# Attention of a two-layer streaming encoder: packed queries, two jobs on their own rows of the array, values stationary in column halves, a negated minimum as the exponent's bias

## The reference, cut to what matters

```python
# A: 6 query heads of 64, 2 key heads, window of 128 tokens, a learned sink per head
m = jnp.maximum(s.max(-1, keepdims=True), sink)
e = jnp.exp(s - m)
p = e / (e.sum(-1, keepdims=True) + jnp.exp(sink - m))
# B: 4 heads, two softmax maps per head of 32 columns each, values of 64
p = jax.nn.softmax(jnp.where(mask, s, NEG_INF), axis=-1)
w = p[:, :, 0] - lam * p[:, :, 1]
o = rms_norm(jnp.einsum('bhqk,bkhe->bqhe', w, v), subln) * (1.0 - lam_init)
# C: 6 heads of 64, causal, logits plus a difference of cumulated forget gates
s = s + (cum_q[..., :, None] - cum_k[..., None, :])
p = jax.nn.softmax(jnp.where(mask, s, NEG_INF), axis=-1)
```

## Time and profile before

| | us |
|---|---|
| three timed executions | 3512.90, 3514.46, 3520.23 (median 3514.46) |
| span of the profiled execution | 3514.1 |
| PE busy in it | 3223.0 (92%) |
| PE weight loads busy | 2884.4 (82%) |
| DVE busy | 1718.7 (49%) |
| ACT busy | 1076.7 (31%) |
| POOL busy | 54.3 (2%) |

### The profile page before, as it was taken

How to read it: one execution, slowest core, us unless ns; L and a number is a source line. 1 busy time by engine, 2 the same in 40 slices (tenths; PEclk the granted TensorE clock), 3 DMA queues, 4 the chain that set the end, 5 groups by cost and what they waited for, 6 DMA issues and landing times. The chain is left out here.

```text
span 3514.1 us, 50348 instructions
## 1 busy us (share of the span) xinstructions
PE 3223.0 (92%) x18146; PEld 2884.4 (82%) x18146; DVE 1718.7 (49%) x4094; ACT 1076.7 (31%) x2321; POOL 54.3 (2%) x32
## 2 busy tenths in 40 slices
PE   0699899998899999999969997999898999999999
PEld 0589777786789999999958896777777999999998
DVE  0444378643244544545445445785434454454454
ACT  1332276553221111111123225665423111111111
POOL 0000010000000000000000001010000000000000
PEclk9899999998999999999989998999998999999999
DMA  7244544333021111111024445525132111111111
GB/s 170 79 138 133 161 122 106 88 82 116 18 66 36 41 49 36 53 37 36 24 92 124 132 136 138 131 69 137 35 94 59 44 36 54 36 36 54 36 36 60
DMA packets 368396, 274.96 MB, mean 78 GB/s; under 512 B 128546, under 2 KB 336366, under 8 KB 368186
## 3 DMA queue, kind: packets, MB, share of 16 engines
q1 hardware_dynamic: 368218, 272.70, 27.5%
HBM read 195.84 MB, written 78.62 MB: 78 GB/s over the span
## 5 line engine op out<-in xcount | busy, mean ns | idle before, releaser
L1515 DVE TENSOR_TENSOR x<-x,ffn_down 128x512 f32<-128x512 f32 x792 | 509.4, 683 | 0.0
L1537 DVE TENSOR_TENSOR ffn_xn<-ffn_xn,ffn_up 128x384 f32<-128x384 f32 x132 | 73.1, 554 | 758.1 <-ACT ffn_xn L1482 758.1
L418 PE MATMUL ffn_up<-ffn_h_hi,ffn_hi_g 128*128 128x384 f32 x1056 | 360.3, 341 | 15.2 <-DVE ffn_h_lo L243 10.5
L419 PE MATMUL ffn_up<-ffn_h_lo,ffn_hi_g 128*128 128x384 f32 x1056 | 359.7, 341 | 0.0
L420 PE MATMUL ffn_up<-ffn_h_hi,ffn_lo_g 128*128 128x384 f32 x1056 | 359.4, 340 | 0.0
L418 PE MATMUL ffn_up<-ffn_h_hi,ffn_hi_u 128*128 128x384 f32 x1056 | 355.2, 336 | 3.2 <-DVE ffn_lo_u L243 3.2
L420 PE MATMUL ffn_up<-ffn_h_hi,ffn_lo_u 128*128 128x384 f32 x1056 | 354.8, 336 | 0.0
L419 PE MATMUL ffn_up<-ffn_h_lo,ffn_hi_u 128*128 128x384 f32 x1056 | 354.8, 336 | 0.0
L991 PE MATMUL att_S<-att_kT,att_qT 128*128 128x512 f32 (+3 forms) x864 | 322.9, 490 | 33.1 <-DMA att_qT<-scratch_qkT 25.9
L1482 ACT ACTIVATE ffn_xn<-ffn_up 128x384 f32<-128x384 f32 x132 | 64.9, 491 | 861.1 <-PE ffn_up L420 861.1
L418 PE MATMUL prj_acc<-prj_w_hi,prj_h_hi 128*128 128x384 f32 (+2 forms) x864 | 318.8, 369 | 0.0
(11 more groups left out here) (173 smaller groups left out, 5352.5 us busy)
## 6 DMA issues: line engine op xcount, KB each, us to landing
ffn_raw_g<-in_w_gate SPq DMA_DIRECT2D x44, 512.0 KB, 4.0
ffn_raw_u<-in_w_up SPq DMA_DIRECT2D x44, 512.0 KB, 5.1
ffn_raw_d<-in_w_down SPq DMA_DIRECT2D x44, 512.0 KB, 5.1
scratch_qkv<-prj_nat SPq DMA_DIRECT2D x72, 192.0 KB, 1.9
prj_w_raw<-in_w_in SPq DMA_DIRECT2D x64, 192.0 KB, 2.6
scratch_qkv<-prj_nat SPq DMA_DIRECT2D x36, 256.0 KB, 2.1
att_kT<-scratch_qkT SPq DMA_DIRECT2D x16, 576.0 KB
att_vn<-scratch_qkv SPq DMA_DIRECT2D x16, 576.0 KB, 8.4
```

Of the source, the lines that this page charges most:

```text
L418: pe.matmul(out, l_hi, r_hi, start=first, stop=False)
L419: pe.matmul(out, l_hi, r_lo, start=False, stop=False)
L1515: dve.tensor_tensor(x, x, down[:, (q * ND + n) % 4, :], ALU.add).then_inc(added, 1)
L1537: dve.tensor_tensor(a32[:, b, :], sg[:, b, :], up[:, b, 1, 0:384], ALU.mult).then_inc(gated, 1)
```

## The change

`Group` pairs become `Step`s. A step holds two jobs: in A and C the two heads of a query tile, in B the two maps of one head. A group has 9 steps in A and C and 18 in B. Step u does what unit u did, in the same iteration pattern; `values` runs once per query tile (a pair) for both heads.

- Queries are packed: `qT` holds one copy, the two jobs' queries on rows 0 to 63 and 64 to 127 (in B on quarters of 32 rows). Nothing is padded and POOL's clearing of `qT` is gone.
- `score` (L1070) multiplies each job on its own rows alone, alternating between the two jobs by chunk of 512 columns, into different banks of `S`. A step of up to 512 columns uses one half of each buffer, so that two such steps fit; a larger one waits for all earlier reductions.
- The mask in C takes four products on half the rows (L1078) where each pair of jobs had two.
- `values` (L1147): a 128x64 block of `vn` is stationary, the 128 columns of `pT` stream, the two heads alternate and write to partitions 0 to 63 and 64 to 127 of `O`. The output is born transposed.
- The normalization moves: POOL copies the inverse sums to 64 columns per head (`widen`, L1018), PE transposes that (L1112), DVE copies it (L1290) and multiplies `O` by it (L1269 `finish`), in chunks of 4, 4 and 1 tiles. The final transposes, their copies, and the whole detour of the sample tile are gone. B's norm is done in the same layout (L1116, L1121, L1216, L1314).
- The reduction stores minus the biased score and takes a minimum, whose start is minus the sink; the result is the exponent's bias as it stands (scale -1 in the exponent). In A a constant column beside the scores makes the sink's term part of the sum. `s` has four buffers.
- The past keys' copies move from ACT to DVE (L1286).
- SP: four more constant loads at the phase's start; the store of a group's output is issued one group later, behind the loads.

```diff
+        self.heads = (0, 1) if h is None else (h, h)
+        self.turned = 2 if h is None else 1
+        self.blocks = [(r, x) for r in range(self.turned) for x in range(g.n_blocks(i))]
+        self.chunks = -(-len(self.blocks) // 4)
+        self.left = 300 * g.j + 2 * P - self.n if g.kind == "A" else 0
+        self.sinks = 1 if g.kind == "A" else 0
...
+    for st in steps:
+        big = st.n > 512
+        half.append(0 if big or not half or steps[st.index - 1].n > 512 else 1 - half[-1])
+        before_it.append(max((x.index for x in steps[:st.index] if big or x.n > 512 or half[x.index] == half[-1]), default=-1))
+
+    def scores(st, r):
+
+        at = half[st.index] * 512
+        return S[:, r, at:at + st.n]
...
+                    for m in range(2):
+                        sp.dma_start(qT[m * HEAD:(m + 1) * HEAD, b, :], t["qkT"][g.q_row(m):g.q_row(m) + HEAD, :]).then_inc(sem, 16)
+                else:
+                    sp.dma_start(qT[:, b, :], t["qkT"][g.q_row(0):g.q_row(0) + P, :]).then_inc(sem, 16)
...
+            def store(g):
+                if g.kind == "B":
+                    sp.wait_ge(sub_done, 3 * (g.j + 1))
+                else:
+                    sp.wait_ge(finished, 3 * (g.index + 1))
+                sp.dma_start(t["mixT"][g.tile * P:(g.tile + 1) * P, :], mixT[:, g.index % 2, :]).then_inc(mix_stored[g.index % 2], 16)
...
-            for b in range(2):
-                pool.memset(qT[:, b, 0:2, :], 0.0).then_inc(q_zeroed[b], 1)
-            for g in groups:
+            def zero_past(g):
                 if g.index:
-                    pool.wait_ge(scored, jobs_to[g.index * UG])
+                    pool.wait_ge(scored, 2 * first[g.index])
                 pool.memset(qpast[:], 0.0).then_inc(qpast_zeroed, 1)
-                if 1 <= g.index < NG - 1 and fresh(groups[g.index + 1]):
-                    pool.memset(qT[:, (g.index + 1) % 2, :, :], 0.0).then_inc(q_zeroed[(g.index + 1) % 2], 1)
+
+            def widen(g, c):
+                a, e = CHUNKS[c]
+                number = 3 * g.index + c
+                by = 2 if g.kind == "B" else 1
+                at = 2 * pairs[g.index * T + a][2][0].index
+                each_head = inv[:, at:at + 2 * by * (e - a):by].unsqueeze(2).broadcast_to([P, 2 * (e - a), HEAD])
+                pool.wait_ge(inv_ready, chunk_end(g, c) + 1)
+                if number >= 2:
+                    pool.wait_ge(turned, place["spread", (number - 2) // 3, (number - 2) % 3] + 1)
+                pool.tensor_copy(wide[:, number % 2, 0:(e - a) * P].rearrange("p (x d) -> p x d", d=HEAD), each_head).then_inc(widened, 1)
...
+                if before_it[u] >= 0:
+                    pe.wait_ge(biased, 2 * before_it[u] + 2)
...
-                    out, q = S[:, job % 2, :], qT[:, b, m, i * P:(i + 1) * P]
-                    if i < TP:
-                        k0, n = g.keys(i)[0] * P, g.n_cols(i)
-                        for c in range(0, n, 512):
-                            w = min(512, n - c)
-                            last = pe.matmul(out[:, c:c + w], q, kT[:, b, k0 + c:k0 + c + w], start=True,
-                                             stop=not (g.kind == "C" and c + w == n))
-                        if g.kind == "C":
-                            last = pe.matmul(out[:, n - P:n], ident_b[:], mask_b[:], start=False, stop=True)
...
+                k0 = g.keys(i)[0] * P
+                for c in range(0, st.n, 512):
+                    w = min(512, st.n - c)
+                    final = c + w == st.n
+                    for r, m in enumerate(st.maps):
+                        rows_of = slice(m * g.D, (m + 1) * g.D)
+                        made = pe.matmul(scores(st, r)[:, c:c + w], qT[rows_of, b, i * P:(i + 1) * P],
+                                         kT[rows_of, b, k0 + c:k0 + c + w], start=True, stop=not (g.kind == "C" and final))
+                        if final and g.kind != "C":
+                            made.then_inc(scored, 1)
...
+                    for part in range(2):
+                        for r in range(2):
+                            rows_of = slice(r * HEAD, (r + 1) * HEAD)
+                            made = pe.matmul(scores(st, r)[:, st.n - P:st.n], ident_b[rows_of, part, :], mask_b[rows_of, part, :],
+                                             start=False, stop=(part == 1))
+                            if part:
+                                made.then_inc(scored, 1)
 
...
+                def out(h):
+                    return O[h * HEAD:(h + 1) * HEAD, number % 2, at:at + P]
+
+                def weights(h, x):
+                    block = x + h * g.n_blocks(i)
+                    return pT[:, pair % 2, block * P:(block + 1) * P]
...
-                        last = pe.matmul(O[:, u % 2, 0:HEAD], pT[:, u % 2, x * P:(x + 1) * P], vn[:, b, kt, v],
-                                         start=(x == 0), stop=(x == len(ks) - 1))
+                        for h in range(2):
+                            made = pe.matmul(out(h), vn[:, b, kt, h * HEAD:(h + 1) * HEAD], weights(h, x),
+                                             start=(x == 0), stop=(x == len(ks) - 1))
...
-                    act.wait_ge(bias_ready, job + 1)
-                    act.activation(p[:, u % 3, r, 0:n], s[:, job % 2, 0:n], ACT.Exp, bias=bias[:, job:job + 1],
-                                   accum_out=total[:, job:job + 1]).then_inc(exped, 1)
-                    if g.kind == "A":
-                        head = g.j + 3 * h
-                        act.activation(esink[:, job:job + 1], sink[:, head:head + 1], ACT.Exp, bias=bias[:, job:job + 1]).then_inc(sink_ready, 1)
+                    act.wait_ge(turned, place["p", u - 3, steps[u - 3].chunks - 1] + 1)
+                for r in range(2):
+                    job = 2 * u + r
+                    act.wait_ge(biased, job + 1)
...
-                    dve.tensor_tensor_reduce(s[:, job % 2, 0:n], S[:, job % 2, 0:n], extra_row, 1.0, -3e38, ALU.add, ALU.max, mx[:, one]).then_inc(biased, 1)
-                    dve.wait_ge(biased, job + 1)
-                    if g.kind == "A":
-                        head = g.j + 3 * h
-                        dve.tensor_scalar(bias[:, one], mx[:, one], sink[:, head:head + 1], -1.0, ALU.max, ALU.mult).then_inc(bias_ready, 1)
-                    elif g.kind == "B":
-                        dve.tensor_scalar(bias[:, one], mx[:, one], -1.0, None, ALU.mult).then_inc(bias_ready, 1)
-                    else:
-
-                        own = k["cumq"][:, i, 2 * g.j + h:2 * g.j + h + 1]
-                        then(dve.tensor_tensor(mx[:, one], mx[:, one], own, ALU.add))
-                        dve.tensor_tensor(bias[:, one], own, mx[:, one], ALU.subtract).then_inc(bias_ready, 1)
...
+                    if u >= 2:
+                        dve.wait_ge(exped, job - 3)
+                    h = st.heads[r]
+                    extra_row = (add_s[:, b, h, 0:st.n] if i == TP else add_p[:, b, h, 0:st.n] if g.kind == "C"
+                                 else add_p[:, b, h, g.width - st.n:g.width])
+                    floor = neg_sink[:, g.j + 3 * h:g.j + 3 * h + 1] if g.kind == "A" else 3e38
+                    dve.tensor_tensor_reduce(s[:, job % 4, st.left:st.left + st.n], scores(st, r), extra_row, -1.0, floor,
+                                             ALU.add, ALU.min, nmax[:, one]).then_inc(biased, 1)
...
+                if c == 0 and g.index >= 2:
+                    dve.wait_ge(mix_stored[g.index % 2], 16 * (g.index // 2))
+                dve.wait_ge(multiplied, g.index * T + e)
+                dve.wait_ge(dve_took, taken[place["spread", g.index, c]])
+                dve.tensor_tensor(mixT[:, g.index % 2, a * P:e * P], O[:, number % 2, 0:(e - a) * P],
+                                  spread[:, number % 2, 0:(e - a) * P], ALU.mult).then_inc(finished, 1)
```

476 lines of the change are left out of this document (251 added, 225 removed).

## The result

Measured side by side, the changed kernel takes 3418.7 us (median of 4 runs, 3416.8 to 3429.1), the kernel before 3514.9 (3512.9 to 3520.2): a ratio of 0.973, 95% interval 0.972 to 0.975. The forecast was 3420. The profiled execution spans 3415.4 us against 3514.1. Its two attention phases run from 411.06 to 785.64 (374.6 us; 419.6 before) and from 2077.48 to 2447.61 (370.1; 419.9). That is 95 us of the 99.

A forecast was written before the change was run, and what follows sets the result against it. PE was taken to bound every group, with DVE close behind in B alone. Group sums gave 372.6 us per layer against 419.6, 47 less, 94 in both layers, taking the profiled 3514.1 to 3420; range 3345 to 3515.

The forecast's parts named there:

- staircase, 2k + 1 passes for k pairs: On PE: one job's second pass runs beside the other's first; C scores 10.5 us (15.4 before), A scores 4.8.
- rival 2: Pairs overlap fully, both passes and the weight loads too; 30 us per layer, 3360; chance 0.20.
- The factor of 1.10: In A: measured 25.94 us against summed product prices of 23.6, applied to the new sum of 22.4, giving 24.7.
- the shape changes: On PE: three per step at 0.12 us each (bounds 0 and 0.2); 3.4 us per A or C group.
- C0's 4 us over C1: In the first C group: 4 us longer than C1, read as B1's last values; C0 forecast at 49.6.
- the late keys: At B0: its keys, issued behind A2's other loads, land after PE wants them; +3 us per layer (0 to 6).
- The loop of scores and two reductions: In B: the next score waits until both reductions are read; 4.85 us at 1024 columns, 64 per group.
- Rival 3: PE, freed, starves: one gap at two A group borders and at B0, 18 us per layer, 3456; chance 0.15.
- the 4 us for constants: At the start: four more loads and some 18 instructions stand before the first reduction; +4 us (2 to 6).
- The tail: After C2: no turning back of the last sample tile and no nine final transposes; -3 us (-4 to 0).
- Rival 1: Products side by side do not overlap and shape changes come on top; 18 us per layer slower, 3549; chance 0.13.
- theory 3: From the B experiments: rows times busy time hold the full clock; with shortened waits 3345 to 3360 us.

The follow-up runs named there:

- loads_reordered: The changed kernel with SyncE issuing the next group's past keys first, then the A or C store, front loads, past values and q; 3394.6 us, ratio 0.966.
- padded_early_start: b_padded with the missed zero rows cleared and only the sinks loaded and awaited before the first reduction; 3358.1 us, ratio 0.954.
- scores_same_rows: The changed kernel with both score and mask products of A and C steps on rows 0 to 63; 3503.8 us, ratio 0.998.
- b_rows64: The changed kernel with B's score products reading 64 rows each instead of 32 (sums over wrong rows); 3379.1 us, ratio 0.962.
- c_rows32: The changed kernel with C's score and mask products on 32 rows each instead of 64 (half the head); 3426.5 us, ratio 0.973.
- b_padded: loads_reordered with B's score products on 64 rows each, q padded with zeros in the other map's 32 rows; 3360.6 us, ratio 0.957.
- b_short_reduction: loads_reordered with the second reduction of B steps over 512 columns done over 512 only (second map wrong); 3390.0 us, ratio 0.962.

## Why the prediction was right, and where it was not

Its total for a layer, 372.6, stands against 374.6 and 370.1. That it met the time is luck: two errors of more than 20 us per layer cancelled. By its own steps, in the first layer:

- **A: 87.5 predicted, 73.9 measured** (32.9, 20.5, 20.5). The step that failed is that two jobs overlap like a staircase, 2k + 1 passes for k pairs. They overlap fully (scores 3.2 for my 4.8, values 0.22 per pair for 0.24), which was rival 2. The factor of 1.10 taken from before was wrong here too: a round takes 1.81, its products alone 1.31, and the shape changes 0.50, not my 0.36 times 1.10 on everything. The change of A2 to the length of A1, without the clearing of `qT` and the 3.11 us wait, came as forecast.
- **C: 154.1 predicted, 146.1 measured** (39.9, 45.1, 61.1). C1 met 45.7 with 45.1, since its scores and values were 4 us cheaper than I had them, its shape changes dearer (0.20 and twice 0.15), and TensorE waits in it for ScalarE's evictions in pieces of 0.25 to 0.47 us, which I had at nothing. The 8.0 come from C0, 39.9 for my 49.6, less 2.3 in C2 with the tail. I had carried C0's 4 us over C1 along as B1's last values. That reading was wrong: in the earlier trace rows both have 404 records, and C0's surplus is idle time and a clock of 0.97. In the change a step of C takes both heads and one of B a single head, so B1 leaves less behind: C0 holds 57 transposes of weights and 92 records of values where C1 has 79 and 144. At 0.11 each and 0.22 for four records of values that makes 5.3 us; the two differ by 5.2.
- **B: 131 predicted with the late keys, 154.5 measured.** This step failed most. The loop of scores and two reductions was right in kind: TensorE waits for `att_nmax` as said. Its size was near wherever the clock held: with 64 rows and transfers on time B0 takes 57.8 and B1 64.9 for my 64 each, the less for scores of 1.99 where I had 2.1 and for pairs in full. What I had not put into it is the clock. I had taken 1.00 from the earlier trace rows, where every score product used all 128 rows. Padding and loads together take 32 us out of B0 and B1 per layer (154.5 to 122.7).
- **Late transfers at B0: +3 predicted, 12 us per layer by loads_reordered.** I followed the keys alone. SyncE's queue holds the store of the group before last behind the front loads, and VectorE, not TensorE, waits for it. Rival 3 named this border, the gap and the fall of the clock, with 18 per layer for three borders; it was one border.
- **Start and tail.** Start and A0 were to go from 35.3 to 38.1 and came at 32.9: of the 4 us for constants, 3.7 are there, as padded_early_start shows, but A0's own steps became cheaper by more. The tail was to become 3 us shorter, 13.1 from the end of C2's last scores to the next phase, and became longer, 18.1 (767.5 to 785.64; 16.1 before). The last steps now hold three query tiles of both heads: 36 transposes of weights and 84 records of values stand behind the last scores. I had counted only what went away there.

So 21.6 us of gain in A and C that I had not counted and 23.5 of loss in B cancelled. (Rival 2 would have had 23 of gain there; that its sum is as near owes something to C0, which it priced like mine.) With both losses in B cured the kernel comes to 3360.6, the 3360 of rival 2. Rival 1 (no overlap) is excluded by scores_same_rows, which takes the overlap from the scores alone and comes back to within 0.4% of the time before.

Shown is that the rows at work decide how soon the full clock returns after a fall, in B (b_rows64 against the changed kernel) and in C0 (c_rows32 and scores_same_rows against the changed kernel), that in B0 they also decide whether it falls (loads_reordered against b_padded), and that late transfers add to it.

What stays open is what else it takes for the clock to fall. B's steps leave TensorE waiting in between, C's hardly do: in the first layer of c_rows32 TensorE is busy for at least 4.17 us in every 5 (taken from each us on) of C1 and C2, against 3.50 ahead of the fall in loads_reordered. So the C runs say nothing on 32 rows together with waits, and theory 3 is neither shown nor excluded; the short reduction did not reach the waits ahead of the fall. And a B pair stands on rows 0 to 63 or 64 to 127 alone, while C's 32-row pair stood on 0 to 31 and 64 to 95. None of these runs separates the two.

The Trainium skill (TensorE: Matmul & The Clock Gate, Part 3) has 3.07 times the rate for four row tiles and 2.38 for three column tiles, both short of the count. Here a pair runs at 2.0 times, of 64 rows since 1.06 - 0.20 became 0.64 - 0.20, of 64 columns since 0.44 per block became 0.22. The Trainium skill (TensorEngine Tiling (Array Packing), Key Properties) says that a change of tiling mode drains the engine. The 0.20 and 0.15 us here agree with it; the 0.20 goes when the change goes.

## What to carry to other kernels

Where two small products can stand on their own rows or their own columns, issue them in turn: a pair costs one product, and a change of shape 0.15 to 0.2 us. Before shrinking products that had been padded, ask what the padding did for the clock: here 64 rows with zeros in half of them cost the same columns as 32 and were worth 34 us in all. When the clock has fallen, look at how long it stays down and at the products that run meanwhile, and not only at the gap that took it. When TensorE gets faster, follow every transfer in the queue to the engine that waits for it, stores from a reused buffer too.

## What the runs showed of the hardware that I had not expected

- Side by side is complete for pairs, including the two passes of a float32 product: 1.99 us for two jobs of 1024 columns, 1.94 for one before.
- Column halves issued job by job cost the same up to two blocks (0.66 either way), and each further block costs 0.44 instead of 0.22.
- A granted clock of 0.50 (1.2 GHz), once reached in B0, lasts 58 us with 32-row products although TensorE is busy for 53 of them, and 17 with 64-row products behind the same stall. In C0 it lasts 3.4 us with 128 rows at work (6.8 once, in b_short_reduction) and 10 to 14 with 64, be they two jobs of 32 or one of 64.
- With 64 rows per job B0 keeps 1.00 (2.4 GHz) with TensorE busy for 3.58 of 5 us. C1 with 32-row products keeps 1.00 even with its scores issued twice, TensorE hardly waiting.
- 18 products of 2 columns in a row go with a fall of the clock in C0 in most runs, though TensorE is busy for 4.75 of the 5 us ahead of it in the changed kernel. No run takes them out, so the cause isn't shown.
- Rows that hold only zeros count as rows at work (b_padded, padded_early_start).
- The same 32-row steps need different times within one execution: B1 takes 81.4 and 72.8 us in the two layers of c_rows32, whose four executions lie between 3404.5 and 3442.2, the widest spread of all runs here.
